# A fused two-block network on one core: the attention slots in another order, a second buffer for the second map, and one normalisation left to the norm behind it

## The chip, the cores and the metric

The kernel runs on one core of one Trainium2 chip, in one launch. A time is the device time of that core in microseconds (us). Of the kernel before, three runs were timed; a fourth execution was recorded by the profiler, and every row below comes from that one.

## The reference, cut to what matters

Two blocks follow each other on a sequence of 512 tokens with 1024 features, in float32. The first has spatial gating, a forgetting attention and a convolutional feed-forward part; the change leaves its arithmetic alone. The second block mixes two groups: a gated delta rule (4 heads) and a differential attention (4 heads, each with two maps of width 64). The change is in the second:

```
def diff_attention_group(...):                      # 4 heads, 2 maps each
    q, k = rmsnorm(q, q_gain) * 64 ** -0.5, rmsnorm(k, k_gain)
    lam = exp(sum(lq1 * lk1)) - exp(sum(lq2 * lk2)) + lambda_init
    def block(q_blk, start):                        # 128 queries at a time
        s = einsum('bqhcd,bkhcd->bhcqk', q_blk, k)
        p = softmax(where(mask, s, neg), axis=-1)
        wts = p[:, :, 0] - lam * p[:, :, 1]
        return einsum('bhqk,bkhv->bqhv', wts, v)
    o = rmsnorm(o, out_gain) * (1.0 - lambda_init)  # over 128 values of a head
    return o * silu(z)

def rmsnorm(x, gain):
    return x * rsqrt(mean(x * x, axis=-1) + EPS) * gain
```

If the first map is left unnormalised, every query's output is too large by the factor s1, the sum of its first exponentials; the rmsnorm behind it takes the factor out again, provided EPS is multiplied by s1 squared.

## The kernel before, in words

Activations lie transposed (features in partitions). Every weight product is a float32 product made of three: the weights and activations are split into a high and a low part, and TensorE (PE) multiplies high by high, high by low and low by high (line 591, function `three`). Weights come in units of 512 KB through a ring of four slots; SyncE loads the raw unit, GpSimd's queue the high part, and VectorE (DVE) makes the low part (`ring_low`, line 1519). All engines walk through one list written out in advance, `MIX2_ORDER`, and each takes from it the entries that concern it, in that order; semaphores join them. So an entry's place in the list is its place in every engine's stream.

The stretch that matters is the differential attention. `_attention(4)` lays out 19 slots; n counts the 16 pieces of work (head h = n // 4, query block i = n % 4, and 128 (i + 1) keys, so widths of 128, 256, 384 and 512 columns in turn). Four kinds of entry belong to a piece:

- **A, scores and maxima.** PE computes both maps' scores (`df_scores`, line 994) into one of two pairs of PSUM banks. DVE masks each and takes its row maximum (`masked_max`, line 1857). ScalarE (ACT) takes the exponential of each, with the row sum as a second output (line 1425): the first map into `P0`, which has three buffers, the second into `PB`, which has one.
- **D, difference.** DVE makes the reciprocals of both sums (line 1866), scales the first map (line 1868), forms -lambda over the second sum (line 1869), and adds the scaled second map (line 1870).
- **B, transposes.** PE transposes the i + 1 blocks of the result into bank 6 (`df_turn`, line 1005) and ACT copies them to `PT2` (line 1435).
- **C, values.** Once per head PE multiplies with the values (`df_attend`, line 1013) and ACT copies the result (line 1440).

Slot n holds D(n - 1), A(n), B(n - 2) and, once per head, C behind them. Between them, by an even spread over the flat list, lie twelve z entries: quarters of three weight products (six matmuls of 128x512 each, line 591) that fill PE; and three `ring` entries for DVE. Every fourth quarter ends a tile that DVE takes out of PSUM (line 1511). PE waits in `df_turn` for D of the same piece and for ACT's copy of the piece before.

Behind the attention follow the scans of the delta rule (`sa`, `sb`), with further z quarters, and the output norm: ACT squares a head (`os`, line 1453), PE sums the squares into bank 5 (line 647), ACT takes the root with EPS as bias (`or`, line 1457), DVE the reciprocal (line 1973), and PE spreads it over rows (`og`, line 653) while ACT applies the silu to the gate (`zs`, line 1444) and DVE multiplies (lines 1978, 1981). The entry `or` 0, for the four heads of this attention, stands behind the entries `sa` 4 and `sb` 4 of the scans.

Of the kernel before, what the change touches and what calls it, by code (L numbers as in the profile page):

```python
# [9 lines left out]
ALU = mybir.AluOpType  # L10
# [4 lines left out]
P = 128  # L15
# [3 lines left out]
NB = T // P  # L19
# [113 lines left out]
def _attention(heads, score="A", weigh="D", turn="B", attend="C", ahead=None):  # L133

    slots = []
    for n in range(NB * heads + 3):
        slot = []
        if 1 <= n <= NB * heads:
            slot.append((weigh, n - 1))
        if n < NB * heads:  # L140
            slot.append((score, n))
# [4 lines left out]
        slots.append(slot + (values + turned if ahead else turned + values))  # L146
# [154 lines left out]
def build(nc, x_t, wstream, params, consts, sgw_t, sgb, out_t):  # L301
    with ExitStack() as ctx:
# [10 lines left out]
        def sem(name):  # L313
            return ctx.enter_context(nc.semaphore(name))
# [96 lines left out]
        SU = SM[:, 24:40].rearrange("p (a b) -> p a b", a=2)  # L411
        RC = SM[:, 40:56].rearrange("p (a b) -> p a b", a=2)
# [55 lines left out]
        f_made, f_log, negc_ready = sem("f_made"), sem("f_log"), sem("negc_ready")  # L468
# [29 lines left out]
        o_sq, o_mm, o_rt, o_rc, o_bc, o_made = (sem(n) for n in ("o_sq", "o_mm", "o_rt", "o_rc", "o_bc", "o_made"))  # L498

# [15 lines left out]
        def score_bank(n, c):  # L515
            return PS[2 + 2 * (n % 2) + c]

# [593 lines left out]
        def _(act):  # L1111
# [48 lines left out]
            act.wait_ge(f_made, 1)  # L1160
# [14 lines left out]
            act.wait_ge(negc_ready, 1)  # L1175
# [130 lines left out]
            for what, n in MIX2_ORDER:  # L1306
# [109 lines left out]
                elif what == "A":  # L1416
                    h, i = n // NB, n % NB
                    w = P * (i + 1)
                    for c in range(2):
# [3 lines left out]
                        if c == 1 and n >= 1:  # L1423
                            act.wait_ge(dw_made, n)
                        act.activation(P0[:, n % 3, 0:w] if c == 0 else PB[:, 0:w], score_bank(n, c)[:, 0:w], ACT.Exp,
                                       scale=-1.0, bias=MX[:, h % 2, 2 * i + c:2 * i + c + 1],
                                       accum_out=SU[:, h % 2, 2 * i + c:2 * i + c + 1]).then_inc(dexp, 1)
# [26 lines left out]
                elif what == "or":  # L1454
                    tiles = slice(4 * n, 4 * n + 4)
                    act.wait_ge(o_mm, tiles.stop)
# [15 lines left out]
        def _(dve):  # L1472
# [71 lines left out]
            def layer_norm(stage, b):  # L1544
# [21 lines left out]
            dve.tensor_scalar(FR[0:8, 0, :], FR[0:8, 0, :], par(C_FB, 1, 0, 8), None, ALU.add).then_inc(f_made, 1)  # L1566
# [5 lines left out]
               .then_inc(negc_ready, 1)  # L1572
# [287 lines left out]
            def difference(n):  # L1860
# [3 lines left out]
                rc = RC[:, h % 2, 2 * i:2 * i + 2]  # L1864
                dve.wait_ge(dexp, 2 * n + 2)
                then(dve.reciprocal(rc, SU[:, h % 2, 2 * i:2 * i + 2]))
                p = P0[:, n % 3, 0:w]
                dve.tensor_scalar(p, p, rc[:, 0:1], None, ALU.mult)
                then(dve.tensor_scalar(S1[:, 0:1], rc[:, 1:2], NEGLAM, None, ALU.mult))
                dve.scalar_tensor_tensor(p, PB[:, 0:w], S1[:, 0:1], p, ALU.mult, ALU.add).then_inc(dw_made, 1)  # L1870
# [240 lines left out]
```

## Time and profile before

| What | us |
|---|---|
| Three timed runs | 1009.2, 1011.83, 1005.51 (median 1009.2) |
| The profiled execution, its own time | 1004.42 |
| Span of its trace, first to last instruction | 1002.7 |
| PE busy, share of the span | 950.4 (95%) |
| DVE busy | 564.3 (56%) |
| ACT busy | 302.1 (30%) |
| GpSimd busy | 72.4 (7%) |

The span is 1.7 us shorter than the execution's time. In the timeline of 40 equal slices (25 us each) PE is at 9 tenths or more in most of them; the slices from 802 to 877 us, where the attention of the second block runs, read 8, 7 and 7, and the chain of work that ended last counts 77% of the span on PE, 63% on line 591 alone. A busy matmul engine here is not an engine at its peak, since matmuls are pipelined and their ends are modelled. PEclk in a row is the clock that TensorE was granted, as a share of 2.4 GHz; 0.50 is the lower of its two levels, 1.2 GHz.

### The profile page before, as it was taken

What the parts mean: (1) busy time and instruction counts of PE and PEld (TensorE: products, weight loads), DVE (VectorE), ACT (ScalarE), POOL (GpSimd) and SP (SyncE); (2) the same over time, 40 slices, a digit from 0 to 9 for tenths busy, and PEclk for the clock granted to TensorE, in tenths of its full rate; (3) what the DMA queues carried; (4) which work ended last, traced back from release to release, by engine and by line L of the source; (5) the groups of instructions that cost most, each with busy time, mean ns of one, the idle gap of its engine ahead of it and who ended that gap; (6) DMA issues with size and microseconds to landing.
All of it is one profiled execution on the core that took longest, in us unless ns stands there. A gap on an engine that the chain in (4) does not pass through costs nothing.

```text
span 1002.7 us, 13611 instructions
## 1 busy us (share of the span) xinstructions
PE 950.4 (95%) x4714; PEld 773.8 (77%) x4714; DVE 564.3 (56%) x968; ACT 302.1 (30%) x555; POOL 72.4 (7%) x138
## 2 busy tenths in 40 slices
PE   9998998999999999999999998899999877899998
PEld 7876776788888888888888886787879764478887
DVE  6266447275877776776344345777553647535443
ACT  6143466333222222221011025524112244413310
POOL 0100000010101010010101100000000000000000
PEclk9998999999999999999999999999999999999999
DMA  8765332275565655656556545555443121112354
GB/s 281 223 197 189 119 113 78 84 223 173 191 203 181 201 190 187 206 180 200 187 190 196 182 146 189 169 165 160 117 139 113 60 67 42 42 63 86 109 172 161
DMA packets 49613, 154.83 MB, mean 154 GB/s; under 512 B 9488, under 2 KB 10512, under 8 KB 49312
## 3 DMA queue, kind: packets, MB, share of 16 engines
q1 hardware_dynamic: 22176, 75.70, 23.5%
q0 software_dynamic: 19008, 69.21, 21.2%
q10 hardware_dynamic: 8384, 9.29, 2.9%
q8 instruction: 31, 0.51, 0.2%
q14 instruction: 14, 0.11, 0.0%
HBM read 149.70 MB, written 4.49 MB: 154 GB/s over the span
## 4 chain that ended last, share of the span: by engine, by line
PE 77%; DVE 10%; ACT 4%; DMA 4%; issue 4%; ACTq 0%; DVEq 0%; SPq 0%; POOLq 0%
PE bank L591 63%; DMA HI<-wstream 3%; PE bank L647 2%; DVE LO L1519 2%; PE bank L653 1%; PE bank L749 1%; PE bank L1013 1%; PE bank L725 1%; PE bank L962 1%; PE bank L921 1%; PE bank L739 1%; PE bank L929 1%; DVE KT L1895 1%; PE bank L977 1%; PE bank L982 1%
## 5 line engine op out<-in xcount | busy, mean ns | idle before, releaser
L591 PE MATMUL bank<-GH,HI 128*128 128x512 f32 x720 | 292.7, 407 | 3.6 <-ACT DV L1359 1.4
L591 PE MATMUL bank<-GH,LO 128*128 128x512 f32 x720 | 284.3, 395 | 0.0
L591 PE MATMUL bank<-GL,HI 128*128 128x512 f32 x720 | 284.1, 395 | 0.0
L1519 DVE TENSOR_TENSOR LO<-RAW,HI 128x1024 fp32r<-128x1024 f32 x88 | 107.4, 1221 | 135.2 <-DMA HI<-wstream 134.7
L591 PEld LDWEIGHTS bank<-GH,HI 128*128 128x128 f32 x720 | 137.7, 191 | 33.0 <-issue 2.7
L591 PEld LDWEIGHTS bank<-GH,LO 128*128 128x128 f32 x720 | 137.3, 191 | 30.0
L591 PEld LDWEIGHTS bank<-GL,HI 128*128 128x128 f32 x720 | 137.6, 191 | 25.6
L573 POOL DMA_DIRECT2D HI<-wstream x132 | 69.8, 529 | 905.8 <-PE bank L591 896.4
L1244 ACT ACTIVATE YC<-AB,PAR 128x512 f32<-128x512 f32 x44 | 36.0, 817 | 140.7 <-DVE AB L1666 140.6
L591 PE MATMUL bank<-AH,HI 128*128 128x512 f32 x176 | 69.3, 394 | 0.0
L591 PE MATMUL bank<-AH,LO 128*128 128x512 f32 x176 | 69.0, 392 | 0.0
L591 PE MATMUL bank<-AL,HI 128*128 128x512 f32 x176 | 68.3, 388 | 0.0
L1666 DVE TENSOR_TENSOR AB<-bank,RB 128x512 f32<-128x512 f32 x44 | 30.4, 691 | 47.8 <-PE bank L591 47.8
L1660 DVE TENSOR_TENSOR LO<-RAW,HI 128x1024 fp32r<-128x1024 f32 x44 | 53.6, 1218 | 4.4 <-DMA HI<-wstream 4.3
L591 PE MATMUL bank<-HI,GH 128*128 128x512 f32 x96 | 38.9, 405 | 2.7 <-DVE CB L1511 1.9
L591 PEld LDWEIGHTS bank<-AH,LO 128*128 128x128 f32 x176 | 33.0, 188 | 7.7
L591 PEld LDWEIGHTS bank<-AL,HI 128*128 128x128 f32 x176 | 33.0, 188 | 7.4
L591 PEld LDWEIGHTS bank<-AH,HI 128*128 128x128 f32 x176 | 33.1, 188 | 6.6
L591 PE MATMUL bank<-LO,GH 128*128 128x512 f32 x96 | 38.1, 397 | 0.0
L591 PE MATMUL bank<-HI,GL 128*128 128x512 f32 x96 | 38.1, 396 | 0.0
L1132 ACT ACTIVATE GH<-X,SM 128x512 fp32r<-128x512 f32 x8 | 5.8, 724 | 104.3 <-DVE X L1724 104.3
L1677 DVE SCALAR_TENSOR_TENSOR YC<-AB,PAR,YC 128x512 f32<-128x512 f32 x44 | 33.1, 752 | 6.0 <-DVE YC L1673 0.3
(285 smaller groups left out, 1276.6 us busy)
## 6 DMA issues: line engine op xcount, KB each, us to landing
RAW<-wstream SPq DMA_DIRECT2D x135, 512.0 KB, 3.7
HI<-wstream POOLq DMA_DIRECT2D x132, 512.0 KB, 4.9
X<-x_t SPq DMA_DIRECT2D x8, 256.0 KB, 7.2
NCB<-out_t ACTq DMA_DIRECT2D x1, 2048.0 KB, 10.1
out_t<-X ACTq DMA_DIRECT2D x8, 256.0 KB, 2.1
XR<-out_t ACTq DMA_DIRECT2D x8, 256.0 KB, 2.6
out_t<-XR SPq DMA_DIRECT2D x8, 256.0 KB, 3.3
EG<-out_t ACTq DMA_DIRECT2D x1, 1024.0 KB, 7.9
```

The costliest lines, as they stand in the source:

```text
L573: pool.dma_start(HI[:, s, :], wstream[bass.ds(2 * i + s // 2, 1), :, 1024 * (s % 2):1024 * (s % 2 + 1)] .rearrange("o p n -> p (o n)")).th ...
L591: mm = pe.matmul(out, a, b, start=(first and n == 0), stop=(last and n == 2))
L647: mm = pe.matmul(out[:, n * b:n * (b + 1)], src[:, P * b:P * (b + 1)], groups, start=True, stop=True)
L653: mm = pe.matmul(out[:, P * b:P * (b + 1)], column(b), IDENT, start=True, stop=True)
L725: pe.matmul(PS[2 + e][:, 0:w], q[r, 4 + p, P * i:P * (i + 1)], k[r, p, 0:w], start=(part == 0), stop=False)
L739: mm = pe.transpose(PS[4 + e][:, P * j:P * (j + 1)], P1[:, 2 * (n % 2) + e, P * j:P * (j + 1)], IDENT)
L749: mm = pe.matmul(PS[6][64 * e:64 * e + 64, P * j:T], VB[:, j, P * p + 64 * e:P * p + 64 * (e + 1)], PT1[:, e, j, P * j:T], start=(j == 0), ...
L1244: act.activation(YC[:, gv, :], AB[:, gv, 2:T + 2], ACT.Identity, scale=PAR[:, bass.ds(6 * t + (C_FCW + 3 * gv + 2), 1)], bias=PAR[:, bass. ...
L1519: dve.tensor_tensor(LO[:, u % RING, :], RAW[:, u % RING, :], HI[:, u % RING, :].bitcast(F32), ALU.subtract).then_inc(unit_split, 1)
L1660: dve.tensor_tensor(LO[:, slot, :], RAW[:, slot, :], HI[:, slot, :].bitcast(F32), ALU.subtract).then_inc(unit_split, 1)
L1666: dve.tensor_tensor(AB[:, gv, 2:T + 2], up_bank(G_UP + 2 * tt + gv)[:, :], RB[:, :], ALU.mult)\
L1677: dve.scalar_tensor_tensor(YC[:, gv, :], AB[:, gv, 0:T], PAR[:, bass.ds(6 * t + (C_FCW + 3 * gv), 1)], YC[:, gv, :], ALU.mult, ALU.add).th ...
```

## The change

Slot n now holds, in this order, C (when it is due), B(n - 2), A(n) and D(n - 1). The second map's exponentials go to `PB` for even and `RS` for odd n. D no longer scales the first map: it takes the reciprocal of the second sum alone, multiplies it by the first sum and by -lambda (one instruction on a single column), and adds the scaled second map to the unnormalised first. All heads' sums are kept. At `or` 0 DVE squares the first map's sums, multiplies by 128 EPS and adds PE's sum of squares out of PSUM; ACT takes the root of that from SBUF, without a bias. One semaphore takes over for two in the first block, so that one is free for the new wait.

```
--- before.py
+++ after.py
@@ -135,15 +135,15 @@
     slots = []
     for n in range(NB * heads + 3):
         slot = []
+        if n < NB * heads:
+            slot.append((score, n))
         if 1 <= n <= NB * heads:
             slot.append((weigh, n - 1))
-        if n < NB * heads:
-            slot.append((score, n))
         if ahead and n % NB == 2 and n // NB + 1 < heads:
             slot.append((ahead, n // NB + 1))
         values = [(attend, (n - 6) // NB)] if n >= 6 and (n - 6) % NB == 0 else []
         turned = [(turn, n - 2)] if 2 <= n < NB * heads + 2 else []
-        slots.append(slot + (values + turned if ahead else turned + values))
+        slots.append(values + turned + slot)
     return slots
 
 
@@ -408,8 +408,8 @@
         RCOL = SM[:, 4:8]
         MX1, SU1, RC1 = SM[:, 8:24], SM[:, 24:40], SM[:, 40:56]
         MX = SM[:, 8:24].rearrange("p (a b) -> p a b", a=2)
-        SU = SM[:, 24:40].rearrange("p (a b) -> p a b", a=2)
-        RC = SM[:, 40:56].rearrange("p (a b) -> p a b", a=2)
+        SU = SM[:, 24:56].rearrange("p (a b) -> p a b", a=4)
+        SU0 = SM[:, 24:56:2]
         LP, LE, NEGLAM = SM[:, 56:58], SM[:, 58:60], SM[:, 60:61]
         EA = SM[:, 61:62]
         S1 = SM[:, 62:64]
@@ -465,7 +465,7 @@
         sgw_masked = sem("sgw_masked")
         idr_made, scratch_stored, scratch_landed = sem("idr_made"), sem("scratch_stored"), sem("scratch_landed")
         xs_made = sem("xs_made")
-        f_made, f_log, negc_ready = sem("f_made"), sem("f_log"), sem("negc_ready")
+        f_rows, f_log = sem("f_rows"), sem("f_log")
         gelu_made = sem("gelu_made")
         s_made, max_made, exp_made, p_ready = (sem(n) for n in ("s_made", "max_made", "exp_made", "p_ready"))
         pt_mm, pt_freed, pv_made = (sem(n) for n in ("pt_mm", "pt_freed", "pv_made"))
@@ -496,6 +496,7 @@
         dpt_mm, dpt_freed, dpv_mm, dpv_freed = (sem(n) for n in ("dpt_mm", "dpt_freed", "dpv_mm", "dpv_freed"))
         silu_z = sem("silu_z")
         o_sq, o_mm, o_rt, o_rc, o_bc, o_made = (sem(n) for n in ("o_sq", "o_mm", "o_rt", "o_rc", "o_bc", "o_made"))
+        o_eps = sem("o_eps")
 
         def bank_of(g):
             return PS[g % 2]
@@ -514,6 +515,9 @@
 
         def score_bank(n, c):
             return PS[2 + 2 * (n % 2) + c]
+
+        def second_map(n):
+            return (PB, RS)[n % 2]
 
         def out_tile(t):
 
@@ -1420,11 +1424,13 @@
                         act.wait_ge(dmax, 2 * n + c + 1)
                         if c == 0 and n >= 3:
                             act.wait_ge(dpt_mm, n - 2)
-                        if c == 1 and n >= 1:
-                            act.wait_ge(dw_made, n)
-                        act.activation(P0[:, n % 3, 0:w] if c == 0 else PB[:, 0:w], score_bank(n, c)[:, 0:w], ACT.Exp,
+                        if c == 1 and n >= 2:
+                            act.wait_ge(dw_made, n - 1)
+                        elif c == 1 and n == 1:
+                            act.wait_ge(qn_bc, 4)
+                        act.activation(P0[:, n % 3, 0:w] if c == 0 else second_map(n)[:, 0:w], score_bank(n, c)[:, 0:w], ACT.Exp,
                                        scale=-1.0, bias=MX[:, h % 2, 2 * i + c:2 * i + c + 1],
-                                       accum_out=SU[:, h % 2, 2 * i + c:2 * i + c + 1]).then_inc(dexp, 1)
+                                       accum_out=SU[:, h, 2 * i + c:2 * i + c + 1]).then_inc(dexp, 1)
                 elif what == "B":
                     h, i = n // NB, n % NB
                     if i == 0 and h:
@@ -1453,6 +1459,10 @@
                     act.activation(SQO[:, n % 2, :], out_tile(n), ACT.Square).then_inc(o_sq, 1)
                 elif what == "or":
                     tiles = slice(4 * n, 4 * n + 4)
+                    if n == 0:
+                        act.wait_ge(o_eps, 1)
+                        act.activation(OC[:, tiles, :], OC[:, tiles, :], ACT.Sqrt, scale=1.0 / P).then_inc(o_rt, 1)
+                        continue
                     act.wait_ge(o_mm, tiles.stop)
                     act.activation(OC[:, tiles, :], PS[5][:, NB * tiles.start:NB * tiles.stop]
                                    .rearrange("p (t b) -> p t b", b=NB), ACT.Sqrt,
@@ -1861,13 +1871,12 @@
 
                 h, i = n // NB, n % NB
                 w = P * (i + 1)
-                rc = RC[:, h % 2, 2 * i:2 * i + 2]
                 dve.wait_ge(dexp, 2 * n + 2)
-                then(dve.reciprocal(rc, SU[:, h % 2, 2 * i:2 * i + 2]))
+                then(dve.reciprocal(S1[:, 1:2], SU[:, h, 2 * i + 1:2 * i + 2]))
+                then(dve.scalar_tensor_tensor(S1[:, 0:1], SU[:, h, 2 * i:2 * i + 1], NEGLAM, S1[:, 1:2],
+                                              ALU.mult, ALU.mult))
                 p = P0[:, n % 3, 0:w]
-                dve.tensor_scalar(p, p, rc[:, 0:1], None, ALU.mult)
-                then(dve.tensor_scalar(S1[:, 0:1], rc[:, 1:2], NEGLAM, None, ALU.mult))
-                dve.scalar_tensor_tensor(p, PB[:, 0:w], S1[:, 0:1], p, ALU.mult, ALU.add).then_inc(dw_made, 1)
+                dve.scalar_tensor_tensor(p, second_map(n)[:, 0:w], S1[:, 0:1], p, ALU.mult, ALU.add).then_inc(dw_made, 1)
 
             for what, n in MIX2_ORDER:
                 if what == "ring":
@@ -1969,6 +1978,12 @@
                     evacuate(G_Z + n, U_Z + n, ZT[:, n, :])
                 elif what == "or":
                     tiles = slice(4 * n, 4 * n + 4)
+                    if n == 0:
+                        sums = SM[:, 232:248]
+                        dve.wait_ge(dexp, 32)
+                        then(dve.tensor_tensor(sums, SU0, SU0, ALU.mult))
+                        dve.wait_ge(o_mm, 4)
+                        dve.scalar_tensor_tensor(sums, sums, P * EPS, PS[5][:, 0:16], ALU.mult, ALU.add).then_inc(o_eps, 1)
                     dve.wait_ge(o_rt, n + 1)
                     dve.reciprocal(OC[:, tiles, :], OC[:, tiles, :]).then_inc(o_rc, 1)
                 elif what == "og":
...
```

The new order shows at three places. The first is DVE at the start of the attention, the first two pieces; ISA rows on line 1857 are the masked maximum and the read of its result, `P_110` is `P0`. Before:

```order
L1857 ISA bank,SM<-bank,CON,SM 128x128
L1857 ISA SM 128x1
L1866 RECIPROCAL SM<-SM 128x2
L1868 TENSOR_SCALAR P_110<-P_110,SM 128x128
L1869 TENSOR_SCALAR SM<-SM 128x1
L1870 SCALAR_TENSOR_TENSOR P_110<-PB,SM,P_110 128x128
L1857 ISA bank,SM<-bank,CON,SM 128x256
L1857 ISA SM 128x1
L1857 ISA bank,SM<-bank,CON,SM 128x256
L1857 ISA SM 128x1
L1866 RECIPROCAL SM<-SM 128x2
L1868 TENSOR_SCALAR P_110<-P_110,SM 128x256
```

and now, where the same maximum is on line 1867:

```order
L1867 ISA bank,SM<-bank,CON,SM 128x128
L1867 ISA SM 128x1
L1867 ISA bank,SM<-bank,CON,SM 128x256
L1867 ISA SM 128x1
L1867 ISA bank,SM<-bank,CON,SM 128x256
L1867 ISA SM 128x1
L1875 RECIPROCAL SM<-SM 128x1
L1876 SCALAR_TENSOR_TENSOR SM<-SM 128x1
L1879 SCALAR_TENSOR_TENSOR P_110<-PB,SM,P_110 128x128
L1867 ISA bank,SM<-bank,CON,SM 128x384
L1867 ISA SM 128x1
L1867 ISA bank,SM<-bank,CON,SM 128x384
```

The maxima of piece 1 (128x256) now stand ahead of the difference of piece 0 (128x128), which has three instructions in place of four.

The second is PE in the middle of the first head, between pieces 3 and 6; lines 994, 1005 and 1013 are scores, transposes and values, line 591 is a z quarter. Before:

```order
L994 MATMUL bank<-DK,DQ 128x128 x2
L1005 MATMUL bank<-CON,P_110 128x128 x3
...
L591 MATMUL bank<-GH,LO 128x512
L994 MATMUL bank<-DK,DQ 128x256 x2
L1005 MATMUL bank<-CON,P_110 128x128 x4
L994 MATMUL bank<-DK,DQ 128x384 x2
L1005 MATMUL bank<-CON,P_110 128x128
L591 MATMUL bank<-GH,HI 128x512
```

and now, where scores are on line 998, transposes on 1009, values on 1017 and z quarters on 595:

```order
L1009 MATMUL bank<-CON,P_110 128x128 x3
L998 MATMUL bank<-DK,DQ 128x128 x2
L1009 MATMUL bank<-CON,P_110 128x128 x4
L595 MATMUL bank<-GH,HI 128x512
...
L595 MATMUL bank<-GH,LO 128x512
L998 MATMUL bank<-DK,DQ 128x256 x2
L1017 MATMUL bank<-PT_112,DV 128x512
...
L1017 MATMUL bank<-PT_112,DV 128x128
L1009 MATMUL bank<-CON,P_110 128x128
L998 MATMUL bank<-DK,DQ 128x384 x2
```

The scores of piece 4 (128x128) stood ahead of the transposes of piece 2 (three blocks) and now stand behind them; the scores of piece 5 (128x256) stood ahead of the four transposes of piece 3, and now stand behind these and behind a z quarter.

The third is DVE at `or` 0, behind the scan entry `sb` 4. Before:

```order
L1950 TENSOR_TENSOR VT<-VT,bank 64x4x128
L1956 SCALAR_TENSOR_TENSOR ST<-ST,EG,bank 128x128 x4
L1973 RECIPROCAL SM<-SM 128x16
L1511 TENSOR_TENSOR ZT<-bank,RB 128x512
L1978 SCALAR_TENSOR_TENSOR DQ<-DQ,PAR,ZT 128x512
```

and now:

```order
L1959 TENSOR_TENSOR VT<-VT,bank 64x4x128
L1965 SCALAR_TENSOR_TENSOR ST<-ST,EG,bank 128x128 x4
L1984 TENSOR_TENSOR SM<-SM 128x16
L1986 SCALAR_TENSOR_TENSOR SM<-SM,bank 128x16
L1988 RECIPROCAL SM<-SM 128x16
L1521 TENSOR_TENSOR ZT<-bank,RB 128x512
L1993 SCALAR_TENSOR_TENSOR DQ<-DQ,PAR,ZT 128x512
```

Two instructions on 16 columns come ahead of the reciprocal; ACT's root, which lies between the second of them and the reciprocal, now reads what the second wrote.

## Rows read from the trace of the kernel before

**Rows 1.** Stretch, us; PE, PEld, DVE, ACT, POOL busy; PEclk; DMA share, GB/s.

```profile
818.20:879.10 60.90, 47.75 (x209) 29.48 (x208) 41.15 (x134) 27.05 (x86) 1.05 (x2) 0.94 0.11 35
879.10:1002.70 123.60, 116.47 (x665) 98.42 (x664) 52.40 (x90) 21.47 (x33) 5.28 (x10) 1.00 0.37 120
```

**Rows 2.** Waits in the attention: waiter, releaser, us in total, times, longest.

```profile
DVE SM L1866 <- ACT PB L1425: 8.4, 12, 0.8
DVE bank L1857 <- PE bank L994: 4.7, 3, 2.6
```

**Rows 3.** Groups in the attention: busy us, mean ns, idle before.

```profile
L1870 DVE SCALAR_TENSOR_TENSOR P<-PB,SM,P 128x128 f32<-128x128 f32 (+3 forms) x16 | 8.8, 552 | 0.6
...
L1425 ACT ACTIVATE PB<-bank,SM 128x128 f32<-128x128 f32 (+3 forms) x16 | 8.3, 520 | 0.0
...
L1868 DVE TENSOR_SCALAR P<-P,SM 128x128 f32<-128x128 f32 (+3 forms) x16 | 6.2, 387 | 0.6
```

**Rows 4.** DVE in time: start us, us, instruction, count [idle before].

```profile
820.23 0.17 DVE L1866 RECIPROCAL SM<-SM 128x2 f32<-128x2 f32 x1 [0.60 <-ACT PB L1425]
...
840.71 0.76 DVE L1857 CUSTOM_DVE_ANT_0 bank<-bank,CON,SM 128x512 f32<-128x512 f32 x1 [1.13 <-PE bank L994]
...
841.38 0.76 DVE L1857 CUSTOM_DVE_ANT_0 bank<-bank,CON,SM 128x512 f32<-128x512 f32 x1
...
843.04 0.17 DVE L1866 RECIPROCAL SM<-SM 128x2 f32<-128x2 f32 x1 [0.84 <-ACT PB L1425]
...
843.65 0.21 DVE L1869 TENSOR_SCALAR SM<-SM 128x1 f32<-128x1 f32 x1
...
844.56 0.35 DVE L1857 CUSTOM_DVE_ANT_0 bank<-bank,CON,SM 128x128 f32<-128x128 f32 x1
...
872.37 0.17 DVE L1866 RECIPROCAL SM<-SM 128x2 f32<-128x2 f32 x1 [0.84 <-ACT PB L1425]
```

**Rows 5.** PE in time, in the attention.

```profile
829.30 0.49 PE L994 MATMUL bank<-DK,DQ 64*128 64x128 f32 x4
...
832.96 0.63 PE L1005 MATMUL bank<-CON,P 128*128 128x128 f32 x4 [0.54 <-ACT PT L1435]
833.51 0.92 PE L994 MATMUL bank<-DK,DQ 64*128 64x384 f32 x4
...
835.73 0.47 PE L591 MATMUL bank<-GH,HI 128*128 128x512 f32 x1
...
837.19 2.32 PE L1013 MATMUL bank<-PT,DV 128*128 128x512 f32 x8
839.44 1.13 PE L994 MATMUL bank<-DK,DQ 64*128 64x512 f32 x4
```

**Rows 6.** The table by stretch again, columns as in rows 1.

```profile
826.10:829.30 3.20, 3.15 (x8) 2.14 (x8) 3.16 (x8) 1.27 (x4) 0.00 (x0) 0.50 0.00 0
```

**Rows 7.** PE in time around the two lower stretches.

```profile
826.15 0.66 PE L1005 MATMUL bank<-CON,P 128*128 128x128 f32 x2 [2.23 <-ACT PT L1435]
826.47 0.78 PE L591 MATMUL bank<-GH,HI 128*128 128x512 f32 x1
...
850.13 0.44 PE L1005 MATMUL bank<-CON,P 128*128 128x128 f32 x1 [2.32 <-ACT PT L1435]
```

**Rows 8.** The output norm's root, all engines, in time.

```profile
907.05 0.28 ACT L1457 ACTIVATE SM<-bank,SM 128x16 f32<-128x16 f32 x1
907.34 1.28 ACT L1444 ACT_TABLE_LOAD   x1
908.64 2.19 ACT L1444 ACTIVATE ZT<-ZT 128x512 f32<-128x512 f32 x4
...
913.47 0.24 DVE L1973 RECIPROCAL SM<-SM 128x16 f32<-128x16 f32 x1
...
915.17 1.05 PE L653 MATMUL bank<-CON,SM 128*128 128x128 f32 x8
...
916.09 0.75 DVE L1978 SCALAR_TENSOR_TENSOR DQ<-DQ,PAR,ZT 128x512 f32<-128x512 f32 x1
```

More of the change, by code:

```diff
@@ L137, in _attention @@
         slot = []
+        if n < NB * heads:
+            slot.append((score, n))
         if 1 <= n <= NB * heads:
             slot.append((weigh, n - 1))
-        if n < NB * heads:
-            slot.append((score, n))
         if ahead and n % NB == 2 and n // NB + 1 < heads:
@@ L145, in _attention @@
         turned = [(turn, n - 2)] if 2 <= n < NB * heads + 2 else []
-        slots.append(slot + (values + turned if ahead else turned + values))
+        slots.append(values + turned + slot)
     return slots
@@ L1455, in _ @@
                     tiles = slice(4 * n, 4 * n + 4)
+                    if n == 0:
+                        act.wait_ge(o_eps, 1)
+                        act.activation(OC[:, tiles, :], OC[:, tiles, :], ACT.Sqrt, scale=1.0 / P).then_inc(o_rt, 1)
+                        continue
                     act.wait_ge(o_mm, tiles.stop)
@@ L1863, in difference @@
                 w = P * (i + 1)
-                rc = RC[:, h % 2, 2 * i:2 * i + 2]
                 dve.wait_ge(dexp, 2 * n + 2)
-                then(dve.reciprocal(rc, SU[:, h % 2, 2 * i:2 * i + 2]))
+                then(dve.reciprocal(S1[:, 1:2], SU[:, h, 2 * i + 1:2 * i + 2]))
+                then(dve.scalar_tensor_tensor(S1[:, 0:1], SU[:, h, 2 * i:2 * i + 1], NEGLAM, S1[:, 1:2],
+                                              ALU.mult, ALU.mult))
                 p = P0[:, n % 3, 0:w]
-                dve.tensor_scalar(p, p, rc[:, 0:1], None, ALU.mult)
-                then(dve.tensor_scalar(S1[:, 0:1], rc[:, 1:2], NEGLAM, None, ALU.mult))
-                dve.scalar_tensor_tensor(p, PB[:, 0:w], S1[:, 0:1], p, ALU.mult, ALU.add).then_inc(dw_made, 1)
+                dve.scalar_tensor_tensor(p, second_map(n)[:, 0:w], S1[:, 0:1], p, ALU.mult, ALU.add).then_inc(dw_made, 1)
             for what, n in MIX2_ORDER:
@@ L1971, in _ @@
                     tiles = slice(4 * n, 4 * n + 4)
+                    if n == 0:
+                        sums = SM[:, 232:248]
+                        dve.wait_ge(dexp, 32)
+                        then(dve.tensor_tensor(sums, SU0, SU0, ALU.mult))
+                        dve.wait_ge(o_mm, 4)
+                        dve.scalar_tensor_tensor(sums, sums, P * EPS, PS[5][:, 0:16], ALU.mult, ALU.add).then_inc(o_eps, 1)
                     dve.wait_ge(o_rt, n + 1)
```

27 lines of the change are left out of this document (16 added, 11 removed).

## The prediction, made before the changed kernel was run

> **What bounds the kernel now.** I read the table by stretch first, then the waits, then the timelines of the attention. Behind the attention PE is busy for 116.5 of 123.6 us, so a later start of that part is a later end [rows 1]. In the attention (818.2 to 879.1 us, all of the changed order) PE is busy for 47.75 of 60.9 us and DVE for 41.15, at a mean clock of 0.94: neither is full, and what sets the pace is a loop of dependences between them. The waits name it [rows 2]: DVE waits 12 times, 8.4 us in all, for the second exponential before it can take reciprocals, and 3 times, 4.7 us, for scores. From the first difference, D(0), to the last, D(15), DVE's timeline shows 872.37 - 820.23 = 52.14 us [rows 4]. That is the number to rework.
>
> **The new loop.** DVE now does the maxima of piece n before D(n - 1), as if scores were always there. But PE now does the transposes of n - 2 before the scores of n, and transposes n - 2 need D(n - 2), the last thing that DVE did. So each turn is one chain through both engines: D(j) on DVE, transposes j on PE, scores j + 2 on PE, both maxima j + 2 on DVE, D(j + 1). Only ACT is off it: its exponentials (j + 1) run beside transposes and scores. Its parts, for j mod 4 = 0, 1, 2, 3:
>
> - D(j) until PE may start: reciprocal 0.20, the one-column product 0.25, the wide addition 0.552 on average [rows 3], and 0.06 of signalling (estimate). The 0.20 and 0.25 are the steps of today's small instructions; 843.65 to the next start is 0.24, and 0.17 of reciprocal has 0.03 behind it [rows 4]. With 0.13 per 128 columns in the addition: 0.86, 0.99, 1.13, 1.26.
> - Transposes of j + 1 blocks before scores may start: 0.55 for four (832.96 to 833.51) [rows 5], estimated 0.12 less per block: 0.20, 0.30, 0.42, 0.55.
> - Scores to maximum: 839.44 to 840.71 is 1.27 for 512 columns, that is 1.13 of matmuls and 0.14; for 128 columns 0.49 + 0.14 [rows 4, 5]; 0.21 per 128 columns between. In the order j + 2: 1.06, 1.27, 0.63, 0.84.
> - Two maxima: 0.67 each at 512 columns (840.71 to 841.38) [rows 4], 0.13 less per 128 columns: 1.07, 1.34, 0.54, 0.80.
>
> The turns are 3.19, 3.90, 2.72 and 3.45, together 13.26 us per head. Today's turn is D(n) whole (1.52 at 512 columns, 843.04 to 844.56) and from the first maximum to the reciprocals (2.33, 840.71 to 843.04) [rows 4]; over the four widths these are 4.9 and 7.2, together 12.1 us per head. So the swap costs 1.2 us per head although D is shorter by one wide instruction: its mean of 0.387 less 0.08 of overlap, 0.31 us, sixteen times, is 4.9 us that the new loop has already been given [rows 3].
>
> From D(0) to D(15) there are three heads (39.78), then 3.19 + 3.90, and D(14) to D(15) without scores between (0.98): 47.85 us. To this come, by the new list:
>
> - A z quarter between transposes and scores in three turns (pieces 5, 9, 13): 1.46 each (835.73 to 837.19) [rows 5], less 0.1 for the step that it replaces: +4.1. The other quarters stand behind scores, beside maxima and D, and cost nothing.
> - The values, 2.25 us (837.19 to 839.44) [rows 5], stand ahead of transposes 4, 8, 12. Maxima, D and signalling cover about 1.8 of them: +0.43 three times, 1.3.
> - One weight split for DVE between maxima 14 and D(13), 1.14 us, and the eviction of the first z tile, with its wait 1.2 us: +2.3. Two splits and the other eviction lie beside PE's part.
>
> Sum 55.6 us, with 0.1 for a D(0) behind maxima 1. Less 52.14: +3.5. Behind D(15), the shorter D gives 0.3 back. **The order and the shorter D together: +3.3 us.** That sum has the clock's two low stretches only on the side of before.
>
> **The clock.** PE stood idle for 2.23 and 2.32 us, and just after each the granted clock is 0.50, 1.2 GHz, in the first case from 826.1 to 829.3 [rows 6, 7]. Waits of under 1.2 us, such as that of 0.54 us at 832.96 [rows 5], had no such thing behind them. In the new loop PE waits before every transpose: about 1.2 us before those of pieces 2, 6 and 10, then 0.97 us of transposes and short scores, then 1.9 us before those of 3, 7 and 11. That is 3.1 us idle of 4, more than before either fall, so I expect a fall there, three times. What then runs at 1.2 GHz is four transposes, the z quarter and the scores of pieces 5, 9, 13, which now all lie on the loop. The quarter takes 2.83 us (826.47 to 829.30) [rows 5, 7] for about 1.5, transposes and scores some 0.3 more: 1.6 us each, 4.7 in all. The Trainium skill ("TensorE: Matmul & The Clock Gate", section "What's actually happening") says that "the default state is throttled, and activity releases the throttle"; by that rule the thinner PE work costs clock and the sum is +8.0, without it the sum stays at +3.3. The trace agrees with the rule at the two places named. I take +8.0.
>
> **The smaller edits.** The second buffer for the second map costs and gives nothing: ACT was idle for 0.0 us before those exponentials [rows 3]. More sum columns and the merged semaphore add no instruction. No DMA is issued more; SP's and GpSimd's loads hang on units done, and shift with them. The norm behind: DVE's two instructions on 16 columns are taken at 0.27 us each, as its reciprocal on as many (0.24 and a step). They start at 913.47; root 0.28 and reciprocal 0.24, with signalling, end at 914.6, and PE comes for the result at 915.17 [rows 8]. That cover of 0.55 us is gone if the root needed its table loaded only then (1.28, as the next load): 0.7 us of loss. ACT is tied up until the root: silu's table load and the first silu end at 914.34 + 1.28 + 0.62 = 916.24, where DVE wants it at 916.09; 0.15 us late on DVE, and with the copy behind it late in turn, with PE filled by z quarters. I take 0, bounds 0 and +1. The unseen one-column product on two scalars I bound by the steps of 0.20 and 0.40 us of its neighbours: -0.8 to +2.4 over 16; 0.25 is the nearest row's.
>
> **The sum.** 1004.4 + 8.0 = 1012.4 us against the profiled execution. This one stands 4.8 us under the median of 1009.2, and the profile doesn't say why; on the median I forecast 1017.
>
> **The rivals.**
>
> - *The clock holds*: the loop as above, but falls no more frequent than today, or off the loop. For it: in the later heads splits and evictions break the pattern. Against: today's two falls. +2 to +5, 1011 to 1014.
> - *The thin stretches are worse*: four or five falls, which slow the first scores too, and the norm's delay reaches PE. +11 to +14, 1020 to 1023. For it: PE's waits before pieces 13 and 15 are of about 1.9 us too. Against: the quarters behind the scores.
> - *The swap works as one would wish, faster than before*: PE delivers scores n before DVE is through with D(n - 1), for instance because transposes cost the stream nothing; then the 8.4 us of waiting for exponentials go, and 4.9 us of wide instructions: -13, bounded by PE's 47.75 us of work; 996. It decides from the point where transposes and scores together end within DVE's remaining work. Against it: today DVE waits 4.7 us for scores that stand ahead of the transposes [rows 2], and D(n - 2) is DVE's last work before maxima n, so nothing is left to cover them.
> - *The change doesn't do what it says*: the double buffer lets nothing overlap, as costed; part of all cases.
>
> **Chances and numbers.** The forecast (+6 to +10) has 0.52, the clock that holds 0.18, the worse clock 0.26, the gain 0.04. About 1%, 10 us, is what a measurement of this kernel can tell from no change. All of the worse case and some of the upper edge of mine, with the spread of the median, are over it: slower 0.31, faster 0.04, same 0.65. The time is 1017; the range takes in +0 to +16 around 1009.2, the rest being the gain and the far ends: 1008 to 1025.
>
> **What would show it.** In the new trace: D(0) to D(15) in 60 us in place of 52; no wait of DVE's reciprocals for exponentials (8.4 to near 0), but some 20 us of waits of its maxima for scores; PE's transposes released by the difference and no longer by the copy; the stretch to the first scan product near 69 us in place of 60.9, at a clock of about 0.9 or less, with 3 or 4 low stretches; the norm's spreading on PE without idle time before it. I am wrong if maxima don't wait (then the loop isn't closed), or if PE's falls don't come, and then by 4 to 5 us; a loss behind the attention would be the norm's.

## The result

The changed kernel took 1019.94 us (median of 4 runs, 1019.33 to 1021.25) against 1009.82 us before (4 runs, 1005.51 to 1011.83): ratio 1.012, 95% interval 1.0075 to 1.0164. It is slower by about 10 us, 1% of the whole; the interval excludes a ratio of 1 and reaches to both sides of 1.01. The forecast was 1017 us, with a range of 1008 to 1025.

### The profile page after: what moved, and what is told of

Same layout as the page of the kernel before. It is cut to its first block, busy times and chain, and to the rows that moved or that the text cites. A ratio compares the mean times of both kernels' runs of the same rounds, so it can differ in the third digit from the quotient of the medians.

```text
span 1018.2 us, 13597 instructions
## 1 busy us (share of the span) xinstructions
PE 960.5 (94%) x4714; PEld 778.0 (76%) x4714; DVE 559.3 (55%) x954; ACT 303.5 (30%) x555; POOL 72.7 (7%) x138
## 4 chain that ended last, share of the span: by engine, by line
PE 78%; DVE 10%; DMA 4%; ACT 3%; issue 3%; ACTq 0%; DVEq 0%; SPq 0%; POOLq 0%
PE bank L595 62%; DMA HI<-wstream 3%; PE bank L651 2%; DVE LO L1529 2%; PE bank L1017 1%; PE bank L998 1%; PE bank L753 1%; PE bank L657 1%; PE bank L729 1%; PE bank L743 1%; PE bank L966 1%; PE bank L925 1%; PE bank L1009 1%; PE bank L933 1%; DVE KT L1904 1%
```

## The profile after

The profiled execution has a span of 1018.2 us (its time is 1019.89), 15.5 us over the one before. The table by stretch, columns as in [rows 1], cut at the first scores of the attention and at the first product of the scans:

```profile
0.00:819.98 819.98, 787.20 (x3842) 646.09 (x3842) 471.23 (x744) 253.83 (x437) 66.30 (x126) 0.98 0.52 168
819.98:892.85 72.87, 55.19 (x209) 32.40 (x208) 35.52 (x118) 28.23 (x86) 1.06 (x2) 0.86 0.09 30
892.85:1018.20 125.35, 118.12 (x665) 99.55 (x664) 52.58 (x92) 21.42 (x33) 5.30 (x10) 0.99 0.37 118
```

The attention took 72.87 us where it had taken 60.9 [rows 1] (60.94 by the same two cuts, 818.17 and 879.11): +11.9. DVE is busy for 5.6 us less and everything takes longer all the same. The parts ahead of it and behind it grew by 1.8 us each, 3.6 in all. The clock was low from 161 to 172 us and from 926 to 930 us, where the one execution before had no fall, and not from 689 to 693 us, where that one had one; the first of these lies in a part that the change leaves alone. The medians, with 10 us between them, don't carry all of the 15.5.

The waits in the stretch, to be read against [rows 2]; first DVE, then PE:

```profile
DVE bank L1867 <- PE bank L998: 27.5, 13, 4.4
DVE DK L1858 <- PE bank L871: 0.8, 1, 0.8
```

```profile
PE bank L1009 <- DVE P L1879: 16.3, 11, 2.1
PE bank L1017 <- ACT PT L1441: 0.7, 1, 0.7
PE bank L1009 <- ACT PT L1441: 0.7, 1, 0.7
```

The 8.4 us in which DVE waited for exponentials are gone entirely. In their place DVE's maxima wait 13 times for scores, and PE's transposes 11 times for the difference: two engines that wait for each other in turn. DVE in time, columns as in [rows 4] (reciprocals on line 1875 open a difference):

```profile
822.16 0.16 DVE L1875 RECIPROCAL SM<-SM 128x1 f32<-128x1 f32 x1
...
832.88 0.16 DVE L1875 RECIPROCAL SM<-SM 128x1 f32<-128x1 f32 x1
...
838.53 0.49 DVE L1867 CUSTOM_DVE_ANT_0 bank<-bank,CON,SM 128x256 f32<-128x256 f32 x1 [4.44 <-PE bank L998]
...
839.35 0.16 DVE L1875 RECIPROCAL SM<-SM 128x1 f32<-128x1 f32 x1
...
848.10 0.16 DVE L1875 RECIPROCAL SM<-SM 128x1 f32<-128x1 f32 x1
...
850.88 0.16 DVE L1875 RECIPROCAL SM<-SM 128x1 f32<-128x1 f32 x1
...
868.90 0.16 DVE L1875 RECIPROCAL SM<-SM 128x1 f32<-128x1 f32 x1
...
873.80 0.16 DVE L1875 RECIPROCAL SM<-SM 128x1 f32<-128x1 f32 x1
...
883.48 0.16 DVE L1875 RECIPROCAL SM<-SM 128x1 f32<-128x1 f32 x1
```

D(0) to D(15) is 61.32 us, forecast 60. The turn from D(6) to D(7) is 848.10 to 850.88, 2.78 us where the sum had 2.72. The turn that holds four transposes, a quarter (the six matmuls of 128x512 of a z entry) and scores is seen at both clocks. D(11) to D(12), 868.90 to 873.80, is 4.90 us at full clock, where the sum had 3.45 + 1.36, so 4.8. D(3) to D(4), 832.88 to 839.35, is 6.47 us. PE's rows of these two turns:

```profile
834.15 1.05 PE L1009 MATMUL bank<-CON,P 128*128 128x128 f32 x4 [1.95 <-DVE P L1879]
834.85 0.77 PE L595 MATMUL bank<-GH,HI 128*128 128x512 f32 x1
...
837.69 0.70 PE L998 MATMUL bank<-DK,DQ 64*128 64x256 f32 x4
...
870.17 0.66 PE L1009 MATMUL bank<-CON,P 128*128 128x128 f32 x4 [1.98 <-DVE P L1879]
870.58 0.47 PE L595 MATMUL bank<-GH,HI 128*128 128x512 f32 x1
...
872.14 0.70 PE L998 MATMUL bank<-DK,DQ 64*128 64x256 f32 x4
```

From the quarter to the scores it is 2.84 us in the one and 1.56 in the other: the clock. The wait ahead is the same, 1.95 and 1.98 us, and the clock fell at the end of the one and held after the other. The table shows the four low stretches, within their edges, and PE's rows behind it what the last of them met; the row of 875.37 us is the same product in the kernel before:

```profile
824.20:827.40 3.20, 3.20 (x10) 2.26 (x8) 1.94 (x7) 1.24 (x4) 0.00 (x0) 0.50 0.00 0
834.20:837.60 3.40, 3.40 (x10) 2.45 (x10) 0.00 (x0) 0.60 (x1) 0.00 (x0) 0.51 0.00 0
851.70:858.00 6.30, 5.85 (x16) 3.65 (x17) 2.41 (x7) 0.90 (x2) 0.00 (x0) 0.50 0.00 0
885.30:892.00 6.70, 6.01 (x14) 3.74 (x13) 0.00 (x0) 1.74 (x3) 0.00 (x0) 0.51 0.01 2
```

```profile
884.84 0.63 PE L1009 MATMUL bank<-CON,P 128*128 128x128 f32 x4 [0.67 <-ACT PT L1441]
886.15 4.63 PE L1017 MATMUL bank<-PT,DV 128*128 128x512 f32 x8 [0.69 <-ACT PT L1441]
```

```profile
875.37 2.42 PE L1013 MATMUL bank<-PT,DV 128*128 128x512 f32 x8 [0.69 <-ACT PT L1435]
```

The values of the last head took 4.63 us where they had taken 2.42, behind a wait of the same 0.69 us. From D(15) to the scans it is 883.48 to 892.85, 9.37 us, against 6.74 before (872.37 to 879.11).

Last the norm's root, to be read against [rows 8]:

```profile
927.21 0.17 DVE L1984 TENSOR_TENSOR SM<-SM 128x16 f32<-128x16 f32 x1
927.42 0.17 DVE L1986 SCALAR_TENSOR_TENSOR SM<-SM,bank 128x16 f32<-128x16 f32 x1
927.87 0.25 DVE L1988 RECIPROCAL SM<-SM 128x16 f32<-128x16 f32 x1 [0.28 <-ACT SM L1464]
```

```profile
930.51 1.05 PE L657 MATMUL bank<-CON,SM 128*128 128x128 f32 x8
```

The chain ends at 928.12, 2.4 us before PE comes for it, and no wait stands ahead of the spreading. PE came 1.6 us later than before, counted from the first scan product (37.66 us for 36.06), since most of its two quarters there ran at the low clock. The chain ended 35.27 us behind that product, so 0.8 us of cover would have been left at PE's old pace.

## The experiments

"Stretch" is from the first scores to the first scan product, "clock" the granted clock in it, "turns" D(0) to D(15), all in us and all from the one profiled execution of each kernel, with the falls of the clock that this execution happened to have. "Filled" means with matmuls added whose results nobody reads. Ratios are of whole runs against the kernel before on the same chip.

| Kernel | Ratio (95%) | Stretch | Clock | Turns |
|---|---|---|---|---|
| before | 1 | 60.94 | 0.94 | 52.14 |
| changed | 1.012 (1.0075-1.0164) | 72.87 | 0.86 | 61.32 |
| e1 old order | 0.9997 (0.9975-1.002) | 60.43 | 0.88 | 49.91 |
| e2 scores first | 0.9873 (0.9844-0.9902) | 53.45 | 0.94 | 44.21 |
| e3 changed, filled | 1.0048 (1.0015-1.0082) | 66.70 | 0.97 | 57.94 |
| e4 changed, old difference | 1.012 (1.0086-1.0155) | 79.92 | 0.79 | 68.09 |
| e5 changed, one buffer | 1.0109 (1.0079-1.0139) | 73.72 | 0.86 | 62.36 |
| e6 changed, quarters behind | 1.0116 (1.0032-1.02) | 74.01 | 0.82 | 63.60 |
| e7 scores first, one buffer | 1.0007 (0.9967-1.0048) | 62.78 | 0.84 | 51.89 |
| e9 scores first, bodies of before | 1.0015 (0.9982-1.0048) | 63.90 | 0.86 | 52.84 |
| e10 before, filled | 1.0 (0.9965-1.0035) | 59.60 | 1.00 | 50.79 |
| e12 old order, filled | 0.9933 (0.9901-0.9964) | 57.72 | 0.94 | 49.02 |
| e11 scores first, filled | 0.9888 (0.9846-0.993) | 51.34 | 1.00 | 42.51 |
| e13 e11, old difference | 0.9863 (0.9808-0.9917) | 54.06 | 1.00 | 45.14 |

**e1: the slots of before, the rest changed.**

```
-        if n < NB * heads:
-            slot.append((score, n))
         if 1 <= n <= NB * heads:
             slot.append((weigh, n - 1))
+        if n < NB * heads:
+            slot.append((score, n))
...
-        slots.append(values + turned + slot)
+        slots.append(slot + turned + values)
```

> The changed kernel with the slots of before (difference, scores and maxima, transposes, values); the shorter difference, the second buffer and the norm stay changed. The stretch from the first scores to the first scan product took 60.9 us before and 72.9 us in the changed kernel. Theory 1 (the order closes a loop through both engines, and that is the loss): 57 to 60 us for the stretch, 2 to 4 us less than before in all, since the difference lost 0.31 us sixteen times, and part of it is hidden. Rival (the loss comes from the bodies, the root of the norm that now waits for VectorE above all): stays 5 to 10 us above before. Norm: no idle time of TensorE before its spreading products.

Putting the old order back takes away the whole loss, so the order made it and the bodies (the shorter difference, the second buffer and the norm) did not. The gain of 2 to 4 us that I expected didn't show in the whole, and the stretch missed its 57 to 60: the turns are 2.2 us shorter (49.91 for 52.14), but the stretch only 0.5, at a clock of 0.88 for 0.94.

**e2: scores and maxima, difference, transposes, values.** One line of the change:

```
-        slots.append(values + turned + slot)
+        slots.append(slot + turned + values)
```

> The changed kernel with slots in the order scores and maxima, difference, transposes, values: VectorE still does maxima n ahead of difference n - 1, but TensorE does scores n ahead of transposes n - 2. Theory 1 says that only the place of the transposes ahead of the scores closes the loop: then VectorE finds its scores ready, its waits for exponentials (8.4 us before) and for scores (27.5 us in the changed kernel) both nearly go, the stretch takes 51 to 54 us, and the whole is 7 to 10 us under before. Rival (maxima ahead of the difference are what delays the transposes and so thins TensorE's work): the stretch stays over 65 us.

The stretch came as the theory had it, and this is a version that beats both kernels, by 1.3% against before. So maxima ahead of the difference are harmless, and what stood ahead of the scores is the fault. That is the transposes above all: two turns in four have nothing else there. But the line moves the values as well, from ahead of the scores to behind the transposes, and with them the places of the quarters; no run moves the transposes alone. One part of the expectation failed: DVE's waits for scores did not nearly go, by the line of DVE's waits in the stretch (columns as in [rows 2]):

```profile
DVE bank L1867 <- PE bank L998: 11.0, 8, 3.0
```

The four longest (2.0 to 3.0 us) are ahead of the 128x512 maxima, where PE still has a quarter, and in three of the four the values too, ahead of the scores. The whole gained more than the stretch did (7.5 us): 1.3% is 13 us, and the medians, 998.62 and 1008.08 us, are 9.5 apart. What makes up the rest isn't settled.

**e3: the changed kernel with filling.** A number for each piece n says how many matmuls go ahead of its transposes:

```
+            FILL = {0: 8, 1: 2, 2: 3, 3: 7, 5: 6, 6: 3, 7: 7, 9: 6, 10: 3, 11: 7, 13: 6, 14: 3, 15: 2}
...
+            def fill(n):
+                g = G_Z + z_tile[0]
+                if FILL.get(n):
+                    pe.wait_ge(gemm_freed, g)
+                for _ in range(FILL.get(n, 0)):
+                    pe.matmul(bank_of(g + 1)[:, :], GH[:, 0, 0:P], GH[:, 0, :], start=True, stop=True)
...
             def df_turn(n):
+                fill(n)
```

> The changed kernel with 65 matmuls of 128x512 more whose results nobody reads, put ahead of the transposes in the attention, a little less of them than TensorE waited there. Theory 1 with the clock: the granted clock stays 1.00 in the stretch, which takes 64 to 66 us in place of 72.9 (loop without falls 64.2), and the whole is 3 to 6 us over before. Rival (the low clock lies beside the loop, so it costs little): 70 us or more, as the added work can only delay.

The table by stretch of this kernel, between the same two cuts:

```profile
817.65:884.35 66.70, 62.90 (x273) 39.42 (x272) 35.61 (x118) 28.30 (x86) 1.06 (x2) 0.97 0.10 32
```

PE does 63 matmuls more (the 65 of the expectation were miscounted by two) and is busy for 7.7 us more (62.90 for 55.19), and the stretch is 6.2 us shorter than without them; the ratio falls from 1.012 to 1.0048, with intervals that overlap only from 1.0075 to 1.0082. So the low clock lies on the loop. The four turns that a fall had made longer are seen here at full clock: D(1) to D(2) takes 3.98 us for 4.62, D(3) to D(4) 4.90 for 6.47, D(7) to D(8) 4.90 for 7.05 and D(8) to D(9) 3.58 for 4.18, together 5.0 us less. The stretch is 0.7 us over the expected 66 and the clock wasn't 1.00 throughout: a low stretch begins at 818 us, ahead of the first filling, and makes D(0) to D(1) 1.1 us longer; at D(9) to D(10) the filling itself delays by 0.5.

**e4: the changed kernel with the difference and the norm of before.**

```
-                then(dve.reciprocal(S1[:, 1:2], SU[:, h, 2 * i + 1:2 * i + 2]))
-                then(dve.scalar_tensor_tensor(S1[:, 0:1], SU[:, h, 2 * i:2 * i + 1], NEGLAM, ...))
+                then(dve.reciprocal(rc, SU[:, h % 2, 2 * i:2 * i + 2]))
                 p = P0[:, n % 3, 0:w]
+                dve.tensor_scalar(p, p, rc[:, 0:1], None, ALU.mult)
+                then(dve.tensor_scalar(S1[:, 0:1], rc[:, 1:2], NEGLAM, None, ALU.mult))
...
```

> The changed kernel with the difference and the norm of before (four instructions, both maps scaled), the new order and the second buffer kept. If the difference lies wholly on the loop, each turn is longer by the 0.31 us of the wide instruction: the stretch takes 3.5 to 5 us more than in the changed kernel, 76 to 78 us, 14 to 16 us over before in all. Rival (it is hidden beside TensorE's part of the loop): within 1 us of the changed kernel.

The difference is on the loop: the turns take 6.8 us more. Nine turns ran at full clock and have a like at full clock in the changed kernel or in e3; together they take 2.8 us more, 0.31 each, and over fifteen that is 4.7 (an estimate). The clock (0.79) has the rest, and it took the stretch 2 us over the expected 78. In the whole it shows less than the expected 14 to 16 us over before: 12 by the ratio, 13.6 by the medians. Against the changed kernel, with the same ratio, the runs don't separate it.

**e5: the changed kernel with one buffer.**

```
-            return (PB, RS)[n % 2]
+            return PB
...
-                        if c == 1 and n >= 2:
-                            act.wait_ge(dw_made, n - 1)
-                        elif c == 1 and n == 1:
-                            act.wait_ge(qn_bc, 4)
+                        if c == 1 and n >= 1:
+                            act.wait_ge(dw_made, n)
```

> The changed kernel with one buffer for the second map, so that its exponentials n wait for difference n - 1, which now stands behind maxima n. Theory 1 (the loop runs through the transposes): the exponentials lie beside transposes and scores, so the buffer is worth 1 us at most; the stretch takes 72 to 75 us (72.9 in the changed kernel), 9 to 13 us over before in all. Rival (the new order leans on the buffer): 4 us or more over the changed kernel.

The stretch is 0.85 us longer and the whole no different: in this order the second buffer buys nothing that whole runs can tell. In the turns its price stands at one place, D(14) to D(15), 1.99 us for 0.99; the others differ by their falls alone.

**e6: quarters behind the scores.**

```
+        if x[0] == "z" and out[k - 1][0] == "B" and out[k + 1][0] in ("A", "ring"):
+            at = next(j for j in range(k, len(out)) if out[j][0] == "A")
+            out.insert(at, out.pop(k))
```

> The changed kernel with every z quarter that stood between transposes and scores moved behind the scores. The prediction's sum gave 4.1 us for three such quarters on the loop, so 68 to 69 us for the stretch and 5 to 7 us over before in all. Against it stands a finer count: the moved quarter then delays the values and with them the next transposes, turn by turn, by about as much; by that the stretch stays within 1.5 us of the changed kernel's 72.9.

74.01 us, 1.1 more than the changed kernel, at a clock of 0.82 for 0.86: the 4.1 us of my sum can't be had by moving the quarters. They were counted on the turns to D(4), D(8), D(12); moved, they run into the values, which the next transposes stand behind. The two turns in question are at full clock in both kernels: D(11) to D(12) takes 3.51 us for 4.90, and D(12) to D(13) 6.08 for 4.72, so 9.59 for 9.62 together.

**e7: scores first with one buffer** (the edits of e2 and e5).

> Scores and maxima, difference, transposes, values, with the new difference and norm, but one buffer for the second map. Here exponentials n wait for difference n - 1 behind maxima n, and nothing else is late: theory 1 expects the buffer to be worth 4 us here: the stretch takes 57 to 59 us in place of 53.5, and the whole is 2 to 6 us under before. Rival (the buffer gives nothing in any order): 53 to 54 us, 10 us or more under before.

The buffer that gives nothing in the changed order is worth 9.3 us of the stretch here, 62.78 for 53.45, more than the 4 expected; the clock is 0.84 for 0.94, and waiting and clock aren't separated in it. The seven turns that ran at full clock in both take 24.37 us for 24.03, so nearly all of the loss lies in turns in which the clock was low in one of the two. With one buffer the gain over before is gone (1.0007, where 2 to 6 us under before were expected).

**e9: the kernel before, with maxima n ahead of difference n - 1.**

```
-        if 1 <= n <= NB * heads:
-            slot.append((weigh, n - 1))
         if n < NB * heads:
             slot.append((score, n))
+        if 1 <= n <= NB * heads:
+            slot.append((weigh, n - 1))
```

> The kernel before with one edit: maxima n stand ahead of difference n - 1; its long difference, one buffer, old norm and transposes behind the scores all stay. If order alone carries the gain of the version with the scores first, the stretch takes 53 to 55 us. By theory 1, the exponentials of the second map wait for the difference of four instructions, so it takes 58 to 61 us, within 2 us of before in all.

No difference in the whole, as expected, though the stretch missed its range upward (63.90, at 0.86). With e7 it says that the good order needs the buffer: this kernel and e7, which has the short difference, are level in the whole.

**e10: the kernel before, filled**: `FILL = {1: 7, 3: 2, 4: 4, 6: 2, 7: 1, 8: 5, 10: 2, 11: 1, 12: 4, 14: 4, 15: 2}`.

> The kernel before with 34 matmuls of 128x512 more whose results nobody reads, ahead of those transposes for which TensorE waited. It is the counterpart of the filled changed kernel (66.7 us at a clock of 0.97). Theory (loop plus clock): the two falls in the stretch go, the clock is 1.00 from the first transposes on, and the stretch takes 59 to 60.5 us in place of 60.9; so of the changed kernel's 11.9 us of loss 6 to 7.5 are the loop and the rest is the clock. Rival (the filling itself delays, in both kernels alike): 63 us or more, then the filled pair says little on the clock.

Its table by stretch:

```profile
813.18:872.78 59.60, 54.55 (x244) 33.29 (x243) 41.15 (x134) 27.09 (x86) 1.06 (x2) 1.00 0.11 36
```

Both falls are gone, and so are 1.3 us. All of it is in one turn, D(10) to D(11), 5.00 us for 6.37; the other fall, in D(2) to D(3), had cost nothing (3.79 for 3.80). Before, then, one of two falls lay on the path; the changed kernel's four cost 7.9 us, by the count further on. The two filled kernels are 7.1 us apart (66.70 and 59.60), which bounds what the loop lost from above.

**e12: the slots of before, the rest changed, filled**: `FILL = {1: 4, 2: 3, 4: 4, 6: 2, 8: 5, 10: 2, 12: 4, 14: 4, 15: 2}`.

> The changed kernel with the slots of before, filled in the same manner (30 matmuls). Unfilled it took 60.4 us with three falls or their ends in the stretch. If the shorter difference pays and only the clock took it back, the stretch takes 56.5 to 58.5 us, 2 to 3 us under the filled kernel before; if the bodies give nothing, the two are equal.

1.9 us under the filled kernel before, with one low stretch still at its start, and 0.9933 in the whole. It is what e1 had hidden: the bodies pay about 2 us of the stretch in the old order, and the clock took most of it back. The whole again shows more, 0.7% or 7 us, than the stretch, which is 3.2 us under that of the unfilled kernel before.

**e11: scores first, filled.**

```
+            FILL = {2: 2, 4: 2, 6: 2, 10: 2, 14: 3, 15: 2}
+            KEY_FILL = {2: 6, 3: 3}
             def spread_key(h):
...
+                for _ in range(KEY_FILL.get(h, 0)):
+                    pe.matmul(bank_of(G_Z)[:, :], GH[:, 0, 0:P], GH[:, 0, :], start=True, stop=True)
```

> Scores and maxima, difference, transposes, values, with 26 matmuls more whose results nobody reads: nine ahead of the last two key spreadings, just before the attention, where a fall came in the unfilled version (816 to 823 us), the others ahead of transposes. Unfilled it took 53.5 us and 998.6 us in all. If the fall before the attention goes, the stretch takes 51 to 52.5 us and the whole is 1 to 3 us under the unfilled version; if the filling only delays, it takes 53.5 us or more.

Its table by stretch:

```profile
815.64:866.98 51.34, 48.78 (x223) 29.77 (x222) 34.84 (x118) 27.15 (x86) 1.05 (x2) 1.00 0.13 42
```

The shortest stretch, 2.1 us under the unfilled one and without a fall. Against the filled changed kernel (e3) it is 15.4 us shorter in the turns, 42.51 for 57.94, of which 1.6 are e3's own low stretch and filling: so most of what e2 gained is the order and not the clock. In the whole it can't be told from e2: 997.1 and 998.6 us, ratios 0.9888 and 0.9873 with intervals that overlap. (The filling of the table came out at 13 matmuls ahead of transposes and nine ahead of the key spreadings; the expectation's 26 was miscounted, by four.)

**e13: the same with the old difference and norm** (the edits of e4 on e11).

> The filled version with the scores first (stretch 51.3 us at a clock of 1.00), with the difference and the norm of before in it: four instructions, both maps scaled. It prices the shorter difference where the clock does not disturb. If VectorE's own work sets the pace there, the 0.31 us come back in most of the turns: 53.5 to 56 us for the stretch. If the stretch is bound by TensorE and ScalarE, it is within 1 us of 51.3, and only order and buffer made the gain.

Its table by stretch:

```profile
819.42:873.48 54.06, 49.33 (x223) 29.68 (x222) 39.35 (x134) 26.99 (x86) 1.05 (x2) 1.00 0.13 40
```

At full clock on both sides, the shorter difference is worth 2.7 us of the stretch (2.6 of the turns), 60% of the 4.5 us for which DVE is busy longer (39.35 for 34.84). The whole doesn't show it (0.9863).

## Why the prediction was right, and where it was not

**The bound.** The stretch is a loop of dependences and not a full engine, as said: 63 more matmuls on the busiest engine made it shorter (e3). (The slices of PE from 802 to 877 us in the kernel before read 7, 7 and 8, in this order, and not 8, 7 and 7; nothing hangs on it.)

**The loop.** This is the step that carried the forecast, and it held. Transposes and values behind the scores (e2) take 19 us off the stretch, 15 off the turns where both are filled (e3, e11); the waits turned over as named. Its size: with the falls taken out, the turns of the changed kernel are 61.32 less 5.0 (D(1) to D(2) 0.6 longer than its like at full clock, D(3) to D(4) 1.6, D(7) to D(8) 2.2, D(8) to D(9) 0.6), so 56.3, where the sum had 55.6. Turn by turn, with quarters, values, splits and eviction where the prediction puts them, every one of the fifteen is within 0.13 us of its forecast then: the loop was right in its parts and not by errors that cancel. The filled kernel's 57.94 is an upper bound, since its filling may delay. The filled kernel before has 50.79. So the loop lost 5.3 us against a kernel before without falls (5.5 in the turns, 0.1 ahead of D(0), less 0.3 behind D(15)); the sum's +3.3 stood against one with its 1.3 us of falls, 4.6 in the same terms. The 6 to 7.5 us expected with e10 were too many. (As added up, 3.5 less 0.3 is 3.2; the prediction rounded up.)

**The clock, mis-sized.** "1.6 us each, 4.7 in all" is the term that was too small. (Three times 1.6 is 4.8, a matter of rounding.) The falls took 5.0 us of the turns and 2.9 behind D(15) (9.37 us for 6.42 in the filled kernel), 7.9 in all. The price of one fall in the turn of four transposes was right (4.90 to 6.47, 1.6). The count was not: of the three turns for which a fall was forecast, D(11) had none; the fall at D(7) lasted twice as long and reached the values; one came at 824 us, and one met the last values, which nothing covers. The rows of the kernel before showed falls at two waits of over 2 us, and not which of several like waits meets one: of four waits of 1.95 to 2.12 us in the changed kernel three did, and that of 1.98 us did not. The rule that activity releases the throttle, by which the sum was +8.0 and not +3.3 (the Trainium skill, "TensorE: Matmul & The Clock Gate", section "What's actually happening"), is borne out by e3 and e11: activity alone, added, took the clock from 0.86 to 0.97 and from 0.94 to 1.00.

Together 5.3 and 7.9 less the 1.3 of before are 11.9 us, which is the stretch's whole difference. The forecast had +8.0; the medians gave +10.1, at the border between its case and that of the worse clock. In the profiled pair it is the worse clock that came: four falls, scores among what they slowed, and a stretch within its +11 to +14; only the norm's delay, which it also named, stayed away. That the whole lies 3 us from the forecast is in part luck, since the stretch alone missed by 3.9 us and what made up for it in the medians isn't known.

**The quarters and the values.** Each fitted the turns that it was put on: D(11) to D(12), with its quarter, was 4.90 us for 4.8, and D(8) to D(9), with the values, 3.58 us at full clock (e3) for 3.62. But they don't stand apart (e6): a quarter moved behind the scores isn't saved, it lengthens the turn of the values by as much. The remark that quarters behind scores cost nothing holds only where no values follow.

**The smaller edits.** The second buffer at nothing: right for whole runs in this order (e5), and wrong as a general remark, since it decides in the other (e7). The norm at nothing: right, with no wait ahead of the spreading; the two instructions took 0.17 us each, 0.21 from the first to the second, where 0.27 was taken. The one-column product took 0.22 us, 0.25 to the next start, as in the sum.

**The rival of a gain.** It named its own condition, transposes that cost the stream nothing ahead of the scores, and its 996 us. With the transposes behind the scores, e2 reached 998.6, beside 1008.1 for the kernel before in the same set of runs.

**Open.** Why the whole gains more than the stretch in e2 and e12, and why e13 is no slower than e11 in the whole; the kernel before alone spreads over 998.5 to 1014.3 us in one set of 26 executions, and profiled executions differ in falls far from the attention. No run holds the clock over the whole kernel, which would tell it. Nor does a run part the transposes' place from that of the values, or the buffer's waits from the clock in e7. Which of several like waits meets a fall stays open too.

## What to carry to other kernels

When one list orders all engines, draw each turn as a chain through them: an entry moved to cover a wait on one engine can put that engine's last result ahead of its own next input on another. Send the producer's next work ahead of the entry that needs the consumer's newest result, and only then spend a buffer on it. Here the buffer was worth something only in the good order. Where TensorE waits on a loop, count what a low clock would do to what it runs next, and test it with matmuls that nobody reads.

## What the runs showed of the hardware that was not expected

- Work without use made the changed kernel faster: 63 matmuls of 128x512 put where TensorE mostly waited took the stretch from 72.87 to 66.70 us, and the granted clock from 0.86 to 0.97. The whole fell from 1.012 to 1.0048 of the kernel before, with intervals that just overlap.
- A wait's length did not decide: at a wait of 1.95 us the clock fell to 1.2 GHz, after 1.98 us, with the same instructions around, it stayed at 2.4 GHz. The same kernel can have a fall in one turn and none in its like.
- A fall that starts at 885.4 us, between waits of 0.67 and 0.69 us, made the last head's values nearly twice as long (4.63 us for 2.42 before, behind the same wait of 0.69 us and without a fall).
- What a fall costs hangs on what TensorE runs at that moment: of the two in the attention before, one cost 1.4 us and the other nothing; the four of the changed kernel cost 0.6 to 2.9 us each.
